# A layer stack with two chunked recurrent mixers: the triangle inversion done on 32x32 diagonal tiles, with a separate corner product

## The reference, cut to what matters

```python
    low = jnp.where(strict, jnp.einsum('bhncd,bhnsd->bhncs', kb, k) * decay, 0.0)
    eye = jnp.eye(DN_CHUNK, dtype=jnp.float32)
    tmat = lax.linalg.triangular_solve(eye + low, jnp.broadcast_to(eye, low.shape),
                                       left_side=True, lower=True)
    u = tmat @ vb
    w = tmat @ (kb * jnp.exp(g)[..., None])
    ...
    def step(s, inp):
        q_i, k_i, u_i, w_i, qk_i, gl_i = inp
        v_new = u_i - w_i @ s
        o_i = q_i @ s + qk_i @ v_new
        s = s * gl_i[..., None, None] + jnp.einsum('bhcd,bhce->bhde', k_i, v_new)
        return s, o_i
```

## Time and profile before

| quantity | value |
|---|---|
| median of 3 runs | 6480.66 us (6477.11 to 6486.7) |
| profiled execution, its own time | 6486.38 us |
| its span, first to last instruction | 6484.6 us |
| mean granted TensorE clock | 0.901 of full |
| TensorE matmul busy / weight load busy | 5473.3 us (84%) / 4914.0 us (76%) |
| VectorE / ScalarE / GpSimd busy | 2521.4 / 1883.0 / 614.3 us |

### The profile page before, as it was taken

The page is one execution under the profiler, slowest core; times in us unless marked ns, Lnnn a source line. Parts: engine busy times, 40 slices in busy tenths (PEclk is TensorE's granted clock), DMA queues, the critical chain, the costliest instruction groups (busy, mean ns, idle before and its releaser), DMA issues. The chain is left out here.

```text
span 6484.6 us, 149579 instructions
## 1 busy us (share of the span) xinstructions
PE 5473.3 (84%) x66220; PEld 4914.0 (76%) x66220; DVE 2521.4 (39%) x4363; ACT 1883.0 (29%) x3891; POOL 614.3 (9%) x1064
## 2 busy tenths in 40 slices
PE   6678999969996578699986788779968899995998
PEld 2377888859995356599885677679948688885998
DVE  0232555434333422343422454343453345543333
ACT  1022334332222222322222333232222243333222
POOL 0002223200000000000000322100000223220000
PEclk7787999989997678899998798889989899997999
DMA  9521000012212100122132211112202100001221
GB/s 407 251 104 42 21 24 22 9 47 88 74 45 80 37 21 11 61 77 77 39 123 63 57 42 36 63 52 78 71 32 99 40 14 23 24 9 64 78 74 53
DMA packets 105672, 426.36 MB, mean 66 GB/s; under 512 B 19208, under 2 KB 34824, under 8 KB 74568
## 3 DMA queue, kind: packets, MB, share of 16 engines
q1 hardware_dynamic: 91920, 388.70, 17.2%
q10 hardware_dynamic: 13248, 30.15, 1.2%
HBM read 369.81 MB, written 49.26 MB: 65 GB/s over the span
## 5 line engine op out<-in xcount | busy, mean ns | idle before, releaser
L356 PE MATMUL bank<-src_hi,ring_hi 128*128 128x320 f32 x4032 | 934.9, 314 | 334.9 <-DVE ring_lo L348 334.9
L356 PEld LDWEIGHTS bank<-src_hi,ring_hi 128*128 128x128 f32 x4032 | 686.4, 191 | 338.4 <-issue 338.2
L356 PE MATMUL bank<-src_lo,ring_hi 128*128 128x320 f32 x4032 | 931.2, 313 | 0.0
L356 PE MATMUL bank<-src_hi,ring_lo 128*128 128x320 f32 x4032 | 929.9, 312 | 0.0
L356 PEld LDWEIGHTS bank<-src_lo,ring_hi 128*128 128x128 f32 x4032 | 686.3, 191 | 0.0
L356 PEld LDWEIGHTS bank<-src_hi,ring_lo 128*128 128x128 f32 x4032 | 685.1, 191 | 0.0
L348 DVE TENSOR_TENSOR ring_lo<-ring,ring_hi 128x2048 fp32r<-128x2048 f32 x190 | 435.0, 2289 | 512.1 <-ACT ring_hi L344 511.3
L562 ACT ACTIVATE stage<-bank 128x320 f32<-128x320 f32 x512 | 196.1, 435 | 1398.9 <-PE bank L356 1398.9
L356 PE MATMUL bank<-hidden_hi,ring_hi 128*128 128x320 f32 x2048 | 466.7, 309 | 0.0
L356 PE MATMUL bank<-hidden_lo,ring_hi 128*128 128x320 f32 x2048 | 466.7, 309 | 0.0
L356 PE MATMUL bank<-hidden_hi,ring_lo 128*128 128x320 f32 x2048 | 466.7, 309 | 0.0
(11 more groups left out here) (348 smaller groups left out, 8851.7 us busy)
## 6 DMA issues: line engine op xcount, KB each, us to landing
ring<-w_mlp SPq DMA_DIRECT2D x128, 1024.0 KB, 4.8
mod_ring<-w_mod SPq DMA_DIRECT2D x48, 2048.0 KB, 11.9
ring<-rw_wrkv SPq DMA_DIRECT2D x24, 1024.0 KB, 4.9
ring<-dn_win SPq DMA_DIRECT2D x16, 1024.0 KB, 5.2
rkv<-stage ACTq DMA_DIRECT2D x48, 320.0 KB, 2.2
r_k<-rkv SPq DMA_DIRECT2D x32, 320.0 KB, 3.6
src<-mixed SPq DMA_DIRECT2D x32, 320.0 KB, 8.1
dn_proj<-stage ACTq DMA_DIRECT2D x32, 320.0 KB, 2.2
```

Of the source, the lines that this page charges most:

```text
L356: last = self.nc.tensor.matmul(acc[h][:, 0:HALF], wt[:, n % 2, k, m * P:(m + 1) * P], x[:, k, h * HALF:(h + 1) * HALF], start=first and q ...
```

## The change

With Q = 32, the first four levels work on the 32x32 diagonal tiles alone. The two heads times two diagonal quarters fill the four 32-partition groups; `quads[n]` is the partition group and `own[n]` the columns that belong to it. Each product of a level is now 16 calls (4 `u` times 4 tiles) of 32x32 with 32 moving columns, in place of 8 calls of 64x64 with 64. `y`, `xx` and `x0` are half as wide, so the copies and masks on ScalarE and VectorE move 128 elements a partition in place of 256.

The last level is a corner product: Y is L's off-diagonal corner times the inverse of one quarter (8 calls, two tiles at a time, line `f_low`), VectorE copies it without a mask, and TensorE forms the upper half of `tt`'s columns by an identity product (8 calls) and the corner (8 calls). The left half of `tt` is written by ScalarE at level 3, scaled by a 0/1 column (`TB_EVEN`).

`first_inverse` no longer uses a masked `x0` from GpSimd: it copies and turns `lt`'s diagonal tiles through TensorE (32 calls in place of 8), and VectorE masks both into `x0` in one operation of 256 elements (in place of ScalarE's copy). The delta stage gets the same edits.

```diff
-                        pool.wait_ge(s["lt_ready"], n + 1)
-                        l0 = table[:, TB_L0I:TB_L0I + C].unsqueeze(1).to_broadcast([P, 4, C])
-                        nc.gpsimd.tensor_tensor(x0[:, 1, :, :], lt[:, n % 2, :, :], l0, ALU.mult).then_inc(s["x0t_ready"], 1)
...
+        four = lambda bank: bank[:, 0:4 * Q]
+        quads = [slice(n * Q, (n + 1) * Q) for n in range(4)]
+        own = [slice(n % 2 * Q, (n % 2 + 1) * Q) for n in range(4)]
...
-                    if level == LEVELS - 1 and prepares(t):
-                        act.wait_ge(s["x0_ps"], t + 2)
-                        nc.scalar.copy(flat(x0[:, 0, :, :]), four(x_bank)).then_inc(s["x0_copied"], 1)
...
+                            last = nc.scalar.copy(flat(xx[:, level % 2, 1, :, :]), four(xt_bank))
+                            if level == LEVELS - 2:
+                                last = nc.scalar.activation(tt[:, t % 2, :, 0:Q], four(xt_bank).rearrange("p (u c) -> p u c", u=4),
+                                                            ACT.Identity, scale=table[:, TB_EVEN:TB_EVEN + 1])
+                            last.then_inc(s["xt_copied"], 1)
...
                 def first_inverse(n):
-                    pe.wait_ge(s["x0t_ready"], n + 1)
+                    pe.wait_ge(s["lt_ready"], n + 1)
                     for u in range(4):
-                        for hr in rows:
-                            last = nc.tensor.matmul(x_bank[hr, u * C:(u + 1) * C], x0[hr, 1, u, :], i64[hr, :], start=True, stop=True)
+                        for f, o in zip(quads, own):
+                            nc.tensor.matmul(x_bank[f, u * Q:(u + 1) * Q], lt[f, n % 2, u, o], i64[f, o], start=True, stop=True)
+                    for u in range(4):
+                        for f, o in zip(quads, own):
+                            last = nc.tensor.matmul(x_bank[f, (4 + u) * Q:(5 + u) * Q], i64[f, o], lt[f, n % 2, u, o],
+                                                    start=True, stop=True)
...
                     for u in range(4):
-                        for hr in rows:
-                            last = nc.tensor.matmul(y_bank[hr, u * C:(u + 1) * C], lt[hr, t % 2, u, :], x[hr, 0, u, :],
-                                                    start=True, stop=True)
+                        if level < LEVELS - 1:
+                            for f, o in zip(quads, own):
+                                last = nc.tensor.matmul(y_bank[f, u * Q:(u + 1) * Q], lt[f, t % 2, u, o], x[f, 0, u, :],
+                                                        start=True, stop=True)
+                        else:
+                            for f, f_low in (quads[0:2], quads[2:4]):
+                                last = nc.tensor.matmul(y_bank[f_low, u * Q:(u + 1) * Q], lt[f, t % 2, u, Q:C], x[f, 0, u, :],
+                                                        start=True, stop=True)
...
                 def next_inverse(t, level):
+                    x = x_in(level)
+                    if level == LEVELS - 1:
+                        pe.wait_ge(s["xt_copied"], LEVELS * t + level)
+                        for u in range(4):
+                            for f, o in zip(quads[1::2], own[1::2]):
+                                nc.tensor.matmul(xt_bank[f, u * Q:(u + 1) * Q], i64[f, o], x[f, 1, u, :], start=True, stop=True)
+                        pe.wait_ge(s["y_ready"], LEVELS * t + level + 1)
+                        for u in range(4):
+                            for f, f_low in (quads[0:2], quads[2:4]):
+                                last = nc.tensor.matmul(xt_bank[f, u * Q:(u + 1) * Q], y[f_low, u, :], x[f_low, 1, u, :],
+                                                        start=True, stop=True)
+                        last.then_inc(s["xt_ps"], 1)
+                        return
...
+                    if level == LEVELS - 1 and prepares(t):
+                        dve.wait_ge(s["x0_ps"], t + 2)
+                        near = table[:, TB_L0I:TB_L0I + C].rearrange("p (w c) -> p w c", w=2).unsqueeze(2).to_broadcast([P, 2, 4, Q])
+                        nc.vector.tensor_tensor(x0[:, :, :, :], x_bank[:, 0:8 * Q].rearrange("p (w u c) -> p w u c", w=2, u=4), near,
+                                                ALU.mult).then_inc(s["x0_copied"], 1)
```

More of the change, by code:

```diff
@@ L973, in rwkv_heads @@
         tok = sb("tok", 3, 2, 6 * C)
[L974 removed]
+        tt, y, xs, sa, state = sb("tt", 2, 4, C), sb("y", 4, Q), sb("xs", 2 * C), sb("sa", 2 * C), sb("state", 2 * C)
         dcol = sb("dcol", 2, 2, NCHUNK)
@@ L1315, in next_inverse @@
                         pe.wait_ge(s["xt_copied"], LEVELS * t + level)
[L1316 to L1322, removed]
-                    for u in range(4):
-                        for hr in rows:
-                            last = nc.tensor.matmul(xt_bank[hr, u * C:(u + 1) * C], y[hr, u, :], x[hr, 1, u, :],
-                                                    start=True, stop=True)
+                    for u in range(4):
+                        for f in quads:
+                            last = nc.tensor.matmul(x_bank[f, u * Q:(u + 1) * Q], x[f, 1, u, :], y[f, u, :], start=True, stop=True)
+                    last.then_inc(s["x_ps"], 1)
+                    for u in range(4):
+                        for f in quads:
+                            last = nc.tensor.matmul(xt_bank[f, u * Q:(u + 1) * Q], y[f, u, :], x[f, 1, u, :], start=True, stop=True)
                     last.then_inc(s["xt_ps"], 1)
@@ L2151, in delta_heads @@
         i64 = table[:, TD_I64:TD_I64 + C]
-        four = lambda bank: bank[:, 0:4 * C]
+        four = lambda bank: bank[:, 0:4 * Q]
+        quads = [slice(n * Q, (n + 1) * Q) for n in range(4)]
+        own = [slice(n % 2 * Q, (n % 2 + 1) * Q) for n in range(4)]
         flat = lambda ap: ap.rearrange("p u c -> p (u c)")
```

87 lines of the change are left out of this document (45 added, 42 removed).

## The result

The changed kernel took 6821.35 us (median of 4 runs, 6813.07 to 6836.6) against 6478.89 us (4 runs): a ratio of 1.053, 95% interval 1.0508 to 1.0552. The forecast was 6373 us with a range to 6520, so the sign was wrong and the time lies outside the range. The profiled execution took 6836.6 us (span 6834.8), 350 us more than that of before. A RWKV slot went from 17.9 to 21.8 us where I had forecast 16.8; a delta slot from 26.1 to 27.8. With 80 and 20 slots that is 3.9 x 80 + 1.7 x 20 = 346 us, nearly the whole loss.

The account below looks back on a forecast made before the run. RWKV was taken as bound by TensorE's own stream; delta also waits for results. RWKV -84 us and delta -24 us made -108 from the profiled 6486.4, so 6378, forecast 6373 us against the runs' median, range 6300 to 6520.

Parts of the forecast that it names:

- Term 1: Inversion's matmuls on TensorE: from 7.0 to 4.8 us a slot, saving 2.2 us.
- The sequencer must also deliver them: Instruction delivery to TensorE: about 6 ns an instruction, 12 ns a matmul, running some 0.8 us ahead of the array.
- The bound: Upper bound on a 32x32 matmul's time in sets of four: 12.5 ns, cutting the saving to 0.6 us a slot.
- The array's rate: 32x32 matmuls in sets of four on TensorE: 9 ns each, between bounds 7.9 and 12.5.
- Changes of shape: Switching tile shape on TensorE: 15 changes of 0.10 us, costing 1.5 us a slot in RWKV, 0.2 in delta.
- The mask at 0.29 and the copies at 0.27 us: VectorE's mask of `y` falls from 423 to 290 ns, ScalarE's copies from 372 to 279 ns.
- Term 3: TensorE's waits on `y` at levels 3 and 2 shrink: 0.45 us a slot credited, bounds 0.2 and 0.5.
- The first: Groups of 32: small matmuls slower than four to a set, 6506 us to about 6670 us; chance 0.18.
- The second: Masks, copies and state chain end later than TensorE wants: about 6450 us; chance 0.16 shared with a lower clock.
- The third: Drains and short bursts lower TensorE's granted clock: 6423 us; chance 0.16 shared with gain lost in waits.
- Theory C: For the bfloat16 run: lower clock after waits is the cause by itself, clock still at 0.88 in RWKV.
- Delta: Delta stretch, 20 slots: saving 40 us, counted at 60% because TensorE waits for ScalarE and root chains: -24 us.

Follow-up runs that it names:

- bfloat16: The changed kernel with the inversion's operands (lt, x0, xx, y, identity) in lower precision, one load and one matmul a call; 6269.14 us, 0.9667 of the kernel before.
- the last float32 version: Changed kernel with VectorE transposes replacing transposed products, first inverse on GpSimd and VectorE, level 4's identity product as ScalarE copies; 6358.52 us, 0.9796 of the kernel before.
- the starved kernels: The changed kernel (1.053), it with only first inverse off TensorE (1.0204), and the VectorE-transpose kernel with 80 unused calls a slot (1.0344), against the kernel before.
- the alternating one: Constant-data stream put ahead of the kernel before, 16 times 16 calls of 32x32 then 8 of 64x64; 21.2 us for its six blocks.

## Why the prediction was wrong

**The step that failed** is in Term 1, "The sequencer must also deliver them". The sum had the slot shorter by 1.15 us and it grew by 3.9. I asked how fast the sequencer passes instructions that are already there (6 ns each over 32 of them) and took that, softened by its lead of 0.8 us, for its rate in the long run. I never asked where the instructions come from. That "a burst of 32 to 64 is mostly already queued" may be true of a burst and said nothing of a slot. The trace of before had a warning. The page's instruction queue has 413 packets of 16 KB, and in its RWKV stages they came at a median of 5.0 us and never under 3.42 us. The change takes 5.55 blocks a slot; at 3.42 us each that is 19.0 us, already above the 17.9 that I had named as the point at which I would be wrong, and at the 3.93 measured it is 21.8. My forecast of 16.8 us asked for a block every 3.03 us. The 3.42 was a warning and no limit: in after, single packets come as close as 3.20 us. What a row of them can keep up, 3.7 to 4.0 us, no row of before shows, because nothing there was starved.

**The bound** of 12.5 ns a matmul stood for the same error: it was the sequencer's pace over 32 instructions, not a bound on supply. At 3.95 us for 128 matmuls and their loads the supply's price is 31 ns a matmul, whatever its size, and the range could not hold what no bound of mine priced.

**The array's rate**, 9 ns a matmul: 8.75 measured. **Changes of shape**, 0.10 each: 0.10 to 0.12 a change over both ways. **The mask at 0.29 and the copies at 0.27 us**, in the changed kernel (columns as in the earlier trace rows), and the added ScalarE operation, which took 0.37 instead of 0.28 and kept nobody waiting:

```profile
L1670 DVE TENSOR_TENSOR y<-bank,table 128x128 f32<-128x128 f32 x147 | 42.5, 289 | 187.3 <-PE bank L1318 187.3
...
L1222 ACT COPY h<-bank 128x128 f32<-128x128 f32 x148 | 39.5, 267 | 338.6 <-PE bank L1345 338.6
...
L1226 ACT ACTIVATE tt<-bank,table 128x128 f32<-128x128 f32 x37 | 13.8, 374 | 0.0
```

**Term 3**: the waits for `y` shrank as said (7.9 to 2.0 us in the stretch), but a slot that is longer for another reason would shrink them too, so this doesn't prove the step. In bfloat16, where the supply leaves more room, they are 8.1 us, and 13.8 in the last float32 version, where VectorE has the transposes as well: the 0.45 us that I credited was probably too kind.

**The rivals.** The first had the right sign and the right place, the groups of 32, and the wrong mechanism: groups did not take 0.5 us, they were cut by gaps. It had 0.18 of the chance and priced the slower stream at up to 15.9 ns a matmul; what was measured is twice that. The reading that I drew from the Trainium skill, TensorEngine Tiling (Array Packing), section Instruction Overhead, with 60 cycles a matmul one after another, came to about 7000 us. That is nearer to 6821 than my own sum, but by luck: 8.75 ns from one matmul to the next shows that no such cost falls on them one after another. The second, gain turned into waits, shows in the bfloat16 and the last float32 version, where TensorE is idle longer for `y` and the state than on issue. The third, the clock: the granted clock in RWKV did fall, from 1.00 to 0.89; with fewer gaps it came back to 0.97. It goes with the loss but does not set the pace: a block took 3.96 us at a clock of 0.89, and 3.97 us at 0.93 in the kernel without the first inverse. Theory C, for the bfloat16 run, wanted the clock still at 0.88 there, and it was 0.97.

**Delta** was to gain 24 us and lost 33. TensorE has 5.6 us there for each 256 instructions (21326 in 470 us), so the supply is not its limit on average; still 10 of the 470 us are idle on issue, where before had none, and the granted clock fell from 0.89 to 0.76. Without the first inverse on TensorE the loss is gone, with 7 us on issue and a clock of 0.78. Whether that is its calls in a dense spot, or the mask of `x0` that the change put on VectorE ahead of other work, no run separates; it stays open. The clock alone does not tell the two kernels apart.

## What to carry to other kernels

Count TensorE's instructions, and set the count against the time: a float32 call is four of them (two loads, two matmuls), and over twenty blocks in a row no run here got 256 in less than 3.67 us; the starved kernels got them in 3.93 to 3.97 on average. A change that cuts matmuls into smaller ones can shorten the array's time (here from 7.0 to about 4.7 us a slot) and still multiply the count (911 to 1422); if the new time for 256 falls under that, price it at the count and not at the array. Idle time put down to "issue", in the middle of a group that waits for nothing and 256 instructions apart, is how it looks in a timeline.

## What the runs showed of the hardware

- The supply of instructions: one block of 256 per 3.74 us in the bare stream of 32x32 matmuls, 3.90 us in the alternating one, 3.93 to 3.97 us in the kernels.
- The packet itself is short: 0.6% of 16 engines over 6834.8 us for 612 packets is 1.1 us each. In the starved stream it starts 1.1 us after TensorE has started again, and TensorE starts again 1.3 to 1.6 us after it has landed. What the chip does in these two stretches no trace shows.
- The plain 64x64 float32 stream (3.73 us a block at full clock) stands right at that limit, so the kernel before, at 5.0 us a block, was not far from it.
- The granted clock fell among the gaps. Over the starved stream of 32x32 it was 0.55, near the lower of the two levels (1.2 GHz of 2.4), and the bursts of 128 went from 1.27 to 1.93 us; in the stream of 64x128 that followed it was 0.98. The alternating stream, with gaps of 0.5 to 1.1 us, kept 1.00:

```profile
298.00:322.00 24.00, 12.18 (x851) 11.38 (x851) 0.00 (x0) 0.00 (x0) 0.00 (x0) 0.55 0.02 5
322.00:379.00 57.00, 57.00 (x1031) 56.89 (x1024) 0.00 (x0) 0.00 (x0) 0.00 (x0) 0.98 0.01 2
...
379.00:400.00 21.00, 16.82 (x762) 14.46 (x760) 0.00 (x0) 0.00 (x0) 0.00 (x0) 1.00 0.02 4
```

- Four 32x32 tiles on the diagonal take 35 ns together (4 x 8.75), in float32; in bfloat16 27.5 ns (4 x 0.11 us / 16).
